# Head transposes moved from TensorE to 32x32 blocks on VectorE and ScalarE, with the strided scores one block later

## What is computed

```python
ATT_GROUPS = ((128, 1), (512, 4), (2048, 16))     # window, dilation; 8 heads of 64 each
...
for gi, (window, dilation) in enumerate(ATT_GROUPS):
    hs = slice(gi * ATT_HEADS, (gi + 1) * ATT_HEADS)
    o, lse = dilated_window_attention(aq[:, :, hs], ak[:, :, hs], av[:, :, hs], window, dilation)
    outs.append(o)
    lses.append(lse)
wts = jax.nn.softmax(jnp.stack(lses), axis=0)
```

## Time and profile before

| | us |
|---|---|
| median of 3 runs | 1291.26 (1291.18 to 1291.30) |
| the profiled execution | 1290.67 |
| its span | 1288.9 |
| TensorE busy | 1275.8 (99%) |
| VectorE busy | 880.0 (68%) |
| ScalarE busy | 608.9 (47%) |
| GpSimd busy | 243.1 (19%) |

### The profile page before, as it was taken

The page is one execution under the profiler, slowest core; times in us unless marked ns, Lnnn a source line. Parts: engine busy times, 40 slices in busy tenths (PEclk is TensorE's granted clock), DMA queues, the critical chain, the costliest instruction groups (busy, mean ns, idle before and its releaser), DMA issues.

```text
span 1288.9 us, 16443 instructions
## 1 busy us (share of the span) xinstructions
PE 1275.8 (99%) x6486; PEld 1053.7 (82%) x6486; DVE 880.0 (68%) x1228; ACT 608.9 (47%) x755; POOL 243.1 (19%) x268
## 2 busy tenths in 40 slices
PE   9999999999999999999999999999999999999996
PEld 7888888887888888888888888888778888888885
DVE  6586785775767665865785867867656766567656
ACT  5444444445555544544563444444454655445441
POOL 1322323220420000400003341342122200004000
PEclk9999999999999999999999999999999999999998
DMA  9867768864566565466657577678556656555662
GB/s 343 289 216 238 231 196 252 271 196 133 179 211 180 167 209 181 137 237 195 211 180 241 186 255 236 212 242 278 164 148 210 194 163 197 174 185 193 197 207 90
DMA packets 129261, 264.98 MB, mean 206 GB/s; under 512 B 8808, under 2 KB 8960, under 8 KB 128672
## 3 DMA queue, kind: packets, MB, share of 16 engines
q1 hardware_dynamic: 123840, 247.49, 61.0%
q0 software_dynamic: 3680, 13.28, 2.9%
q10 hardware_dynamic: 1664, 3.16, 0.7%
HBM read 258.61 MB, written 5.28 MB: 205 GB/s over the span
## 4 chain that ended last, share of the span: by engine, by line
PE 98%; DVE 1%; ACT 1%; issue 0%; DVEq 0%; POOL 0%; POOLq 0%; ACTq 0%
PE ps L368 91%; PE ps L482 1%; PE ps L671 1%; PE ps L386 1%; PE ps L639 1%; PE ps L523 0%; PE ps L343 0%; DVE w_lo L1035 0%; PE ps L537 0%; PE ps L560 0%; ACT w_hi L737 0%; PE ps L508 0%; PE ps L654 0%; PE ps L545 0%; PE ps L399 0%; PE ps L690 0%
## 5 line engine op out<-in xcount | busy, mean ns | idle before, releaser
L1035 DVE TENSOR_TENSOR w_lo<-w_raw,w_hi 128x1024 fp32r<-128x1024 f32 x408 | 533.6, 1325 | 323.0 <-ACT w_hi L737 320.8
L737 ACT ACTIVATE w_hi<-w_raw 128x1024 fp32r<-128x1024 f32 x408 | 428.5, 1058 | 478.9 <-PE ps L368 436.8
L368 PE MATMUL ps<-w_hi,xT_hi 128*128 128x512 f32 x1632 | 644.8, 395 | 0.0
L368 PE MATMUL ps<-w_hi,xT_lo 128*128 128x512 f32 x1632 | 636.1, 390 | 0.0
L368 PE MATMUL ps<-w_lo,xT_hi 128*128 128x512 f32 x1632 | 635.4, 389 | 0.0
L368 PEld LDWEIGHTS ps<-w_hi,xT_hi 128*128 128x128 f32 x1632 | 306.4, 188 | 65.0 <-issue 3.0
L368 PEld LDWEIGHTS ps<-w_hi,xT_lo 128*128 128x128 f32 x1632 | 306.3, 188 | 64.7
L368 PEld LDWEIGHTS ps<-w_lo,xT_hi 128*128 128x128 f32 x1632 | 306.6, 188 | 61.4
L287 POOL TENSOR_TENSOR carried<-ident 1x1 f32<-1x1 f32 x30 | 20.4, 678 | 447.4 <-DVE arena L1358 178.7
L1202 DVE CUSTOM_DVE_ANT_0 mix<-xres,mix 128x1024 f32<-128x1024 f32 x64 | 79.8, 1248 | 1.1
L368 PE MATMUL ps<-ahead,xT_hi 128*128 128x512 f32 x184 | 57.1, 392 | 0.0
(11 more groups left out here) (235 smaller groups left out, 777.8 us busy)
## 6 DMA issues: line engine op xcount, KB each, us to landing
w_raw<-w_in_dram SPq DMA_DIRECT2D x368, 512.0 KB, 4.4
w_raw<-w_out_dram SPq DMA_DIRECT2D x64, 512.0 KB, 4.7
mix<-gate_w_dram SPq DMA_DIRECT2D x32, 512.0 KB, 6.2
mix<-x_t_dram SPq DMA_DIRECT2D x8, 256.0 KB, 6.0
xres<-x_dram ACTq DMA_DIRECT2D x4, 512.0 KB, 9.6
v_dram<-arena POOLq DMA_DIRECT2D x4, 512.0 KB, 5.5
z<-v_dram POOLq DMA_DIRECT2D x8, 256.0 KB, 6.6
z<-ln_g_dram POOLq DMA_DIRECT2D x2, 1024.0 KB, 5.9
```

Source lines behind the costliest of these rows:

```text
L368: mm = pe.matmul(ps[2 * s + t][:], a[:, order[c] * KC + k, t * P:(t + 1) * P], b[:, k], start=(c + k + i == 0), stop=(c == CH - 1 and k == ...
L737: A(hi_of(n, c), w_raw[:, c % RING], ACT.Copy).then_inc(w_hi_done, 1)
L1035: TTn(lo_of(n, c), w_raw[:, c % RING], hi_of(n, c).bitcast(F32), ALU.subtract).then_inc(w_lo_done, 1)
```

## The change

Queries of all three groups and keys of the two strided groups are no longer transposed on TensorE. VectorE transposes `z` in 32x32 blocks (`turn`, two instructions of 128x512 per operand) into scratch space `zs`. This leaves each block in the partitions it came from. ScalarE then moves blocks to the partitions they belong to, with 16 copies per operand on 32 partitions by 256 elements (`moved`). In the strided groups the block transpose also writes tokens by residue, elements 8 places (32 bytes) apart. The keys of the third group stay with TensorE. ScalarE makes four moves, then one split, and so on. In the strided groups the scores go from the values' block to after the first chunk of the next block, the probability transposes from the third chunk of that block to the fifth, and the values stay. VectorE now takes the values out of PSUM before the maxima.

```diff
+        zs = [arena[:, 3072 + w * 1024:3072 + (w + 1) * 1024] for w in range(2)]
...
                     chunks(n0, q0, 1, 0, CH)
-                    chunks(n0 + 1, q0 + 1, 0, 0, 5)
-                    head_transposes(0)
-                    chunks(n0 + 1, q0 + 1, 0, 5, CH)
-                    chunks(n0 + 2, q0 + 2, 1, 0, 5)
-                    head_transposes(1)
-                    chunks(n0 + 2, q0 + 2, 1, 5, 7)
+                    chunks(n0 + 1, q0 + 1, 0, 0, CH)
                     if g < NCOMP:
+                        chunks(n0 + 2, q0 + 2, 1, 0, CH)
+                        chunks(n0 + 3, q0 + 3, 0, 0, 1)
                         comp_scores()
-                        chunks(n0 + 2, q0 + 2, 1, 7, 8)
-                        chunks(n0 + 3, q0 + 3, 0, 0, 3)
+                        chunks(n0 + 3, q0 + 3, 0, 1, 5)
                         comp_transposes()
-                        chunks(n0 + 3, q0 + 3, 0, 3, 7)
+                        chunks(n0 + 3, q0 + 3, 0, 5, 7)
                         comp_values()
                         chunks(n0 + 3, q0 + 3, 0, 7, 8)
                         continue
+                    chunks(n0 + 2, q0 + 2, 1, 0, 5)
+                    key_transposes()
+                    chunks(n0 + 2, q0 + 2, 1, 5, 7)
                     scores(0)
...
+                    def moved(which, first, last):
+
+                        act.wait_ge(turned, l * (2 * GROUPS - 1) + g * 2 + which + 1)
+                        for i in range(first, last):
+                            u, f = i // 4, i % 4
+                            src, rows = zs[which][u * 32:(u + 1) * 32], slice(f * 32, (f + 1) * 32)
+                            if g < NCOMP:
+
+                                mv_ = A((qT, kT)[which][rows].rearrange("p m (r t u i) -> p u t (m r) i", r=RES, t=TT, u=4)[:, u],
+                                        src.rearrange("p (t f q i) -> p f t q i", t=TT, f=4, i=8)[:, f], ACT.Copy)
+                            else:
+                                mv_ = A(qT[rows].rearrange("p m (t u s) -> p u t m s", t=TT, u=4)[:, u],
+                                        src.rearrange("p (t f m s) -> p f t m s", t=TT, m=PAIRS, f=4)[:, f], ACT.Copy)
+                        if last == 16:
+                            mv_.then_inc(qkT_act, 1)
...
-                    transposed(0, qT, qTr)
-                    split(n0 + 2, 0, 4)
+                    for i in range(4):
+                        moved(0, 4 * i, 4 * i + 4)
+                        split(n0 + 2, i, i + 1)
...
+                        for i in range(3):
+                            moved(1, 4 * i, 4 * i + 4)
+                            split(n0 + 3, i, i + 1)
+                        moved(1, 12, 16)
                         take(n0 + 3, 1, vS[:, 0])
+                        split(n0 + 3, 3, 7)
                         comp_exponentials()
...
+                    def turn(which):
+
+                        dve.wait_ge(roped, qk + which + 1)
+                        for t in range(TT):
+                            dst, src = zs[which][:, t * BW:(t + 1) * BW], z[:, which, t].rearrange("p (m f s) -> p f m s", m=PAIRS, f=4)
+                            if g < NCOMP:
+
+                                f = V.transpose(dst.rearrange("p (b r i) -> p b i r", r=RES, i=8), src)
+                            else:
+                                f = V.transpose(dst, src)
+                        f.then_inc(turned, 1)
...
-                    transposed(0, qT, qTr)
+                    turn(0)
                     gate_sums(1)
...
+                        turn(1)
+                        split(n0 + 3, 0, 3)
+                        take(n0 + 3, 1, vS[:, 1])
+                        split(n0 + 3, 3, 4)
+                        comp_maxima()
+                        split(n0 + 3, 4, 6)
+                        comp_sums()
```

More of the change, by code:

```diff
@@ L212, in hybrid_layers @@
         own_dve, own_pool, own_act = sem("own_dve"), sem("own_pool"), sem("own_act")
[L213 removed]
+        mask_set, roped, turned = sem("mask_set"), sem("roped"), sem("turned")
         qk_ps, qkT_act, qkT_dve = sem("qk_ps"), sem("qkT_act"), sem("qkT_dve")
@@ L467, in _, with key_transposes @@
                     qk = l * (GROUPS * 2) + g * 2
[L469 to L478 removed]
+                    def key_transposes():
+                        pe.wait_ge(roped, qk + 2)
+                        pe.wait_ge(comp_og_act, comp)
+                        pe.wait_ge(comp_og_dve, comp)
                         for m in range(PAIRS):
@@ L481, in head_transposes @@
                                 at = ((m % 2) * TT + t) * P
-                                tr = pe.transpose(ps[4 + 2 * which + m // 2][:, at:at + P],
-                                                  z[:, which, t, m * P:(m + 1) * P], ident[:])
+                                tr = pe.transpose(ps[6 + m // 2][:, at:at + P], z[:, 1, t, m * P:(m + 1) * P], ident[:])
                         tr.then_inc(qk_ps, 1)
@@ L1231, in _ @@
                     split(n0 + 2, 4, 8)
-                    transposed(1, kT, kTr)
+                    if g < NCOMP:
+                        turn(1)
+                        split(n0 + 3, 0, 3)
+                        take(n0 + 3, 1, vS[:, 1])
[3 more added lines that the diff above has]
+                        comp_sums()
+                        split(n0 + 3, 6, 7)
+                        split(n0 + 3, 7, 8)
+                        comp_prob_copy()
+                        split(n0 + 4, 0, 2)
+                        comp_output_copy()
+                        split(n0 + 4, 2, 4)
+                        continue
+                    keys_copied()
                     split(n0 + 3, 0, 2)
```

65 lines of the change are left out of this document (17 added, 48 removed).

## The result

The changed kernel takes 1311.17 us in the median of 4 runs (1309.2 to 1315.6), the kernel before 1291.28 in the same comparison. The ratio is 1.0158 with a 95% interval of 1.0147 to 1.017: **slower by about 20 us, where 1283.6 was forecast and 1289.0 was the range's upper end.** The profiled execution took 1309.2 us, its span is 1307.5 against 1288.9.

What follows compares the result with a forecast made beforehand. TensorE, busy 99%, was taken as the bound. Nine places saving 0.91 us and one losing 0.54 made 7.65 off 1290.67, 1283.0; with 0.59 for the median, 1283.6 us, range 1282.4 to 1289.0.

Steps and rivals of the forecast that it cites:

- TensorE loses 0.91 us a group: On TensorE, each of ten removed groups of eight head transposes saves 0.91 us, 9.1 us in all.
- The scores later: On TensorE, moving the strided scores, their transposes and values between other chunks was costed at nothing.
- The turn at 0.60 us an instruction: On VectorE, each block transpose takes 0.60 us, 1.2 us an operand; bounds 0.8 and 2.26 us an operand.
- The first rival: On VectorE, the block transpose is slow, 2.26 us an operand, leaving a gain of 4.2 us: 1287.1 us; chance 0.24.
- The moves at 0.30 us: On ScalarE, moves start 0.30 us apart, sixteen per operand; far end 0.496 us if nothing overlapped.
- a move of 0.40: On the key side, moves of 0.40 us end the chain 0.3 us late in four places: 1285 us, inside the range.
- VectorE's gates stay the later of the two for the first chunk: In the values' block, VectorE's gate dot products, not ScalarE's moves, decide the first low part: 73.3, wanted at 73.89.
- the fourth chunk's own use: In the values' block, moves and splits end at 75.4; TensorE wants the chunk at 82.05, VectorE's part needing 1.2 more.
- The sixth place: Query place in layer 1, group 0: the turn takes 1.2 us for 0.66, so TensorE loses 0.54 us there.
- Second rival: ScalarE's moves bound the key chain in four places: measurable loss from 0.54 us a move, about 1298 at 0.60; chance 0.08.
- a chance of 0.08 for slower: For the whole kernel, the probability given to a slower result, beside 0.82 for faster and 0.10 for within 0.2%.

Runs made afterwards that it cites:

- v2: v3 with strided scores, probability transposes and values one chunk or more later, and ScalarE's split ahead of each four key moves: 1282.70 us, ratio 0.9931.
- e4: The kernel before with only the strided scores and what goes with them placed as in the changed kernel; all head transposes on TensorE: 1291.2 us, ratio 1.0.
- e2: The changed kernel with the strided groups' block transposes written contiguously, tokens not sorted by residue: 1303.36 us, ratio 1.0098.
- v3: The changed kernel with query turn halves between VectorE's splits of the keys' block and two query moves behind each of eight splits: 1289.26 us, ratio 0.9988.
- e1: The changed kernel with ScalarE's first four splits of the values' block and the take ahead of the sixteen query moves: 1299.32 us, ratio 1.0062.
- e3: The changed kernel with four moves of 128 partitions per operand instead of sixteen of 32, blocks staying in their partitions: 1286.94 us, ratio 0.9966.
- e5: The changed kernel with VectorE's split of the values' block's fifth chunk ahead of the second four gate dot products: 1311.9 us, ratio 1.015.
- e6: The changed kernel with the same moves on 32 partitions reading and writing contiguous runs, blocks landing in wrong places: 1309.99 us, one run.
- e7: e6 with each move writing the same 32 partitions that it reads: 1293.02 us, one run.
- e9: e7 with each four moves in a row reading 32 partitions and writing the next 32: 1294.94 us, one run.
- e8: The changed kernel with moves reordered: four in a row write the same 32 partitions and read four different ones: 1311.89 us, ratio 1.0156.
- v1: The kernel before with only the queries off TensorE, turn halves between VectorE's splits and two moves behind each of eight splits: 1286.71 us, ratio 0.9962.

## Why the prediction was wrong, step by step

- **TensorE loses 0.91 us a group: right.** 6406 instructions are 80 fewer, and v2, where nearly no wait is left, is 8.6 to 8.8 us faster against 10 x 0.91 - 0.65 = 8.45.
- **The scores later cost nothing: right** (e4).
- **The turn at 0.60 us an instruction: wrong in the strided groups,** right (0.685 long) where the write is contiguous. At 1.13 they lie at the dear end I had bounded, 2.1 us an operand. The first rival had this right, and so had the Trainium skill's rule on lines ("SBUF — State Buffer", SBUF: two separate sides) that stands beside it. I let the PSUM copies with 16-byte steps speak against it, which read strided but do not write so. By e2 this size is worth 8 us.
- **The moves at 0.30 us: wrong.** The neighbours on 128 partitions always address the same partitions. The moves start 0.43 apart, between the ends of 0.30 and 0.496 that I had named. I then said that a move of 0.40 would only make the key chain 0.3 us late: that was worked out with the cheap turn, the two dear terms were never put into one sum. Together they give 88.2 + 2.1 + 16 x 0.43 + 3 x 1.1 = 100.5 against 98.37, 2 us late in four places, and v3 shows 1.4 to 2.0.
- **"VectorE's gates stay the later of the two for the first chunk": true, and with the moves' price the failed step.** I checked the moves against the fourth chunk's own use (75.4, then 82.05), counted a cover of over 5 us, and stopped. But on VectorE the take and four more dot products stand behind that chunk's split, and the fifth chunk's low part behind those. The rows had it: before, that part was done at 83.42 + 1.2 = 84.6, and with 0.91 us won TensorE would want it at 73.89 + 10.88 = 84.8. The cover was 0.2 us. The fourth low part came 2.7 us later than before (81.1 less the late start of 1.0, for 77.4), which leaves 2.5, and TensorE waits 2.39. It is six of the seven waits for splits, 13 of 15.1 us; e1, e3 and e5 show the link from three sides.
- **It took both, the link and the price.** At the prediction's own prices the link costs nothing: moves and splits end at 75.4 and the fourth low part at 76.6, just where VectorE's gates, 0.68 us earlier, would have put it (77.4 - 0.68 = 76.7). In fact the turn took 0.9 us more, and moves and splits 11.2 instead of 8.6: 16 x 0.13, and 1.1 instead of 0.944 for each of the splits, since none overlaps the moves. Taken one at a time from the changed kernel, cheaper moves are worth 17 us (e6 to e7, one run each), the query moves out of the way 12 (e1), a cheap turn 8 (e2). These overlap and do not add up.
- **The sixth place: right in place, short in size.** In layer 1's first group TensorE waits 2.13 us at 721.91, where I had 1.4; the turn is 0.9 dearer than taken.
- **Waits bring the low clock behind them: not in the sum.** The kernel before has no wait of over 1.6 us and no such stretch ahead of its last 8 us, so it showed no price. In the profiled execution of the changed kernel the next wait gives it back, in the median some 2 of the 20 us go with it, in e5's profile 8.6.
- **Second rival (slower by the moves):** its mechanism was real, but it was priced from the scores' side alone, where 0.54 us a move was needed. With the unseen link 0.43 were enough, even with a cheap turn (e2, 1303). So a chance of 0.08 for slower was far too small.

What stays open: what decides whether the clock falls behind a wait, and so why runs of one kernel differ by up to 7 us. Their times follow their granted clocks, but only one execution of each kernel has a profile, so where the others lost them is not shown.

## What to carry to other kernels

When work is put ahead of a step in an in-order stream, follow that step's lateness to everything queued behind it on the next engine, until a use by the bounding engine; the step's own use is only the first check. Put all dear ends of unknown costs that lie in one chain into one sum, not one at a time. A wait, or a slower stretch, costs only what no later wait for another engine gives back. And place the work behind the split that the others need, in small pieces over many chunks: the same instructions at the same prices were 20 us slower in one order and 8.6 us faster in the other.

## What the runs showed of the hardware

- VectorE's 32x32 block transpose of 128x512 float32 takes 0.685 us with contiguous writes and 1.129 with writes 32 bytes apart. The Trainium skill ("SBUF — State Buffer", SBUF: two separate sides) states that crossing its 16-byte lines is penalised; the trace agrees and gives the size for this one pattern, a factor of 1.65. No run tried another distance, so that it is the lines is not shown.
- ScalarE overlaps the end of an instruction with the next (0.31 us apart at 0.40 long) when both address the same partitions, read and written (e3, e7, e9). When either changes, moves stand 0.43 apart (the changed kernel, e6, e8), and a split behind a move on other partitions loses its overlap too. Where only the number of partitions differed and the first was the same (e7, v1, v3), the overlap stayed. One case, e9's take out of PSUM, overlaps though the first partition read is another.
- Two block transposes with strided writes in a row take 2.12 us, so they overlap by 0.14.
- TensorE's granted clock was at half (1.2 instead of 2.4 GHz) behind a part of its long waits, for 3.4 us each time and 6.8 in two places of e5: in the profiles of all these kernels behind none of the waits under 1.7 us, behind 9 of the 27 between 1.7 and 2.2, behind 7 of the 13 between 2.3 and 2.4, and behind all five of 2.9 and over. The matmuls behind took 1.2 to 2.9 us more for it, which is lost only where no later wait gives it back (the changed kernel, e8). The same wait of the same kernel is followed by it in one place and not in another.
